# A hybrid encoder layer on one core: the input projection as seven half-size products, its operands made in the stage before

## What is computed

```python
h = rmsnorm(x, g_mix)                       # x: (2048, 1024)
proj = h @ w_in + b_in                      # w_in: (1024, 2304)
qa = rotary(proj[..., :s1].reshape(b, s, 8, 64), positions)
ka = rotary(proj[..., s1:s2].reshape(b, s, 2, 64), positions)
va, qb, kb, vb = ...                        # the other columns of proj: 128, 512, 512, 512
oa = window_sink_gqa(qa, ka, va, sinks)
ob = chunk_relbias_attention(qb, kb, vb, rel_bias)
mix = concat([rmsnorm(oa, g_grp_a), rmsnorm(ob, g_grp_b)])
x = x + mix @ w_out
x = x + memory_cross_attention(rmsnorm(x, g_cross), rmsnorm(mem, g_mem), w_cq, w_ckv, w_co)
h = rmsnorm(x, g_ffn)
x = x + (silu(h @ w_gate) * (h @ w_up)) @ w_down
out = rmsnorm(x, g_final)
```

## Time and profile before

| | |
|---|---|
| Median of 3 runs | 2958.81 us (2955.07 to 2966.77) |
| The profiled execution | 2957.17 us |
| Its span | 2955.4 us |
| TensorE matmuls, share of the span | 94% |
| `stage_products`, first to last matmul | 16.0 to 129.2 us |
| `stage_qkv`, first to last matmul | 133.7 to 575.2 us |
| Attention, first matmul | 595.4 us |

### The profile page before, as it was taken

The page is one execution under the profiler, slowest core; times in us unless marked ns, Lnnn a source line. Parts: engine busy times, 40 slices in busy tenths (PEclk is TensorE's granted clock), DMA queues, the critical chain, the costliest instruction groups (busy, mean ns, idle before and its releaser), DMA issues. The chain is left out here.

```text
span 2955.4 us, 39417 instructions
## 1 busy us (share of the span) xinstructions
PE 2789.1 (94%) x14112; PEld 2358.7 (80%) x14112; DVE 1601.4 (54%) x2913; ACT 1063.8 (36%) x2101; POOL 1052.2 (36%) x756
## 2 busy tenths in 40 slices
PE   7898999789999899799998799999999998999998
PEld 7787878689999788688887588888788887788876
DVE  3247447357779533233333566667766665655354
ACT  5433333256666322233332333334333332222242
POOL 6644444301000011312121555555555554453152
PEclk9999999989999899899999899999999999999999
DMA  7656666475665433212223433335433333744454
GB/s 237 224 185 216 220 233 220 137 181 138 161 161 122 156 133 135 111 61 75 86 75 120 158 107 99 98 100 177 137 107 107 95 105 120 268 147 140 146 172 129
DMA packets 244536, 428.48 MB, mean 145 GB/s; under 512 B 17792, under 2 KB 151424, under 8 KB 239104
## 3 DMA queue, kind: packets, MB, share of 16 engines
q1 hardware_dynamic: 211040, 364.72, 38.5%
q10 hardware_dynamic: 33312, 61.35, 7.0%
HBM read 285.50 MB, written 135.27 MB: 142 GB/s over the span
## 5 line engine op out<-in xcount | busy, mean ns | idle before, releaser
L50 PE MATMUL gu_acc<-gu_t,shared_m 128*128 128x512 f32 x880 | 344.2, 391 | 8.6 <-DVE gu_t L2348 5.1
L51 PE MATMUL gu_acc<-gu_t,shared_m 128*128 128x512 f32 x880 | 343.5, 390 | 0.0
L52 PE MATMUL gu_acc<-gu_t,shared_m 128*128 128x512 f32 x880 | 343.4, 390 | 0.0
L334 POOL TENSOR_TENSOR front_wq_lo<-front_wq_raw,front_wq_hi 128x1024 fp32r<-128x1024 f32 x72 | 177.8, 2471 | 215.2 <-ACT front_wq_hi L330 214.7
L1424 PE MATMUL att_sum_o<-att_v,att_turned_sb 128*128 128x64 f32 x1616 | 204.2, 271 | 0.0
L50 PEld LDWEIGHTS gu_acc<-gu_t,shared_m 128*128 128x128 f32 x880 | 165.8, 188 | 44.6 <-issue 5.5
L1424 PEld LDWEIGHTS att_sum_o<-att_v,att_turned_sb 128*128 128x128 f32 x1616 | 198.5, 194 | 0.2
L52 PEld LDWEIGHTS gu_acc<-gu_t,shared_m 128*128 128x128 f32 x880 | 165.9, 189 | 34.7
L51 PEld LDWEIGHTS gu_acc<-gu_t,shared_m 128*128 128x128 f32 x880 | 166.0, 189 | 34.3
L1394 PE MATMUL att_sum_s<-att_k,att_q 128*128 128x320 f32 (+3 forms) x704 | 146.7, 328 | 25.1 <-DMA att_k<-qk_d 24.1
L2296 ACT ACTIVATE shared_m<-gu_w_sum 128x512 fp32r<-128x512 f32 x132 | 83.3, 631 | 226.0 <-PE gu_acc L52 210.6
(11 more groups left out here) (310 smaller groups left out, 7335.5 us busy)
## 6 DMA issues: line engine op xcount, KB each, us to landing
front_wq_raw<-in_w_in ACTq DMA_DIRECT2D x69, 512.0 KB, 3.8
down_a<-a_d SPq DMA_DIRECT2D x37, 704.0 KB, 4.1
ahead_w_even<-in_w_gate SPq DMA_DIRECT2D x44, 512.0 KB, 4.4
more_w_odd<-in_w_up SPq DMA_DIRECT2D x44, 512.0 KB, 4.3
a_d<-gu_a_mix SPq DMA_DIRECT2D x88, 256.0 KB, 3.1
att_k<-qk_d SPq DMA_DIRECT2D x36, 512.0 KB, 13.1
a_d<-gu_a SPq DMA_DIRECT2D x66, 256.0 KB, 4.1
shared_m<-a_d SPq DMA_DIRECT2D x19, 704.0 KB, 4.3
```

What stands on the lines that cost most here:

```text
L50: pe.matmul(out, l_hi, r_hi, start=first, stop=False)
L51: pe.matmul(out, l_hi, r_lo, start=False, stop=False)
L52: return pe.matmul(out, l_lo, r_hi, start=False, stop=last)
L334: pool.tensor_tensor(self.lo[:, i % Q_SLOTS, :], self.raw[:, i % Q_SLOTS, :], raw(self.hi[:, i % Q_SLOTS, :]), ALU.subtract).then_inc(self ...
```

## The change

The projection is done by seven products of half depth for a pair of column tiles and half of the tokens (`N_PROD`, `PAIRS_IN`), 18 such pairs in all, 126 products of 12 matmuls. The columns of `w_in` are ordered anew outside of the kernel, so that a rotation pairs results of two tiles (head halves lie in different tiles): the four swap DMAs are gone, GpSimd makes the sine products (`sin_products`), VectorE the cosine products and the sums (`rotate`). GpSimd also makes the sums of weights (`sums`). A pair of weight tiles is loaded once per half of the tokens instead of once per block of 512. The stored q and k have 14 tiles of columns where there were 13.

All sixteen row tiles of x are now prepared in `stage_products`, as whole float32 tiles `prod_h` (no high and low there); VectorE forms four mixtures of each two (`mix_pair`), and the seven operands go to DRAM as `th_d` (56 stores of 256 KB, 24 from ScalarE and 32 from SyncE). They are loaded back in `stage_qkv`, as 14 operands of 1 MB, the first two ahead of its start (`FirstOperands`, which also serves the gate and up stage in place of `GateUpOperands`, with the same operations). The sine and cosine table is made once, in `stage_products`, and stored to `trig_d`. The rows of x have four buffers instead of two; ScalarE issues their loads and the stores of the unmixed operands. `m_d` is stored in rows of 4 KB and read back in four pieces.

```diff
     def load(self, sp, n, rows):
-        if n >= 2:
-            sp.wait_ge(self.s_xn, n - 1)
-        sp.dma_start(self.x[:, n % 2, :], rows).then_inc(self.s_x[n % 2], 16)
+        if n >= self.slots:
+            sp.wait_ge(self.s_xn, n - self.slots + 1)
+        sp.dma_start(self.x[:, n % self.slots, :], rows).then_inc(self.s_x[n % self.slots], 16)
...
-        SQUARE, SCALE, TURN = (2, 6, 24, 40), (3, 7, 28, 41), (5, 14, 34, 43)
-        RSQRT, LOAD = (6, 10, 15, 19), (5, 5, 11, 15)
...
+        def at_share(share):
+
+            whole = sum(cost(a) for a in range(TOTAL))
+            return min(a for a in range(TOTAL) if sum(cost(i) for i in range(a + 1)) >= min(share, 1) * whole)
...
+        def stage_at(j, steps):
+            return at_share((8 + 5.6 * j + steps) / 106)
+
+        TURN = [stage_at(j, 0) for j in range(NT)]
+        SCALE = [stage_at(j, -3) for j in range(NT)]
+        SQUARE = [stage_at(j, -7) for j in range(NT)]
+        WHOLE = [stage_at(j, 2) for j in range(NT)]
+        MIX = [stage_at(2 * i + 1, 5) for i in range(HT)]
+        PUT_MIX = [stage_at(2 * i + 1, 9) for i in range(HT)]
+        AT_ONCE = rows.slots - MT
+        TABLE = [at_share((20 + 4 * part) / 106) for part in range(6)]
+        AHEAD = at_share(0.75)
...
+                def put_mixed(i):
+                    sp.wait_ge(s_mixed, 4 * i + 4)
+                    put(sp, 5, i, h[:, (2 * i + 1) % 4, 0:KH, :], s_plain[i % 2])
+                    for m, q in enumerate((3, 2, 4)):
+                        put(sp, q, i, mixed[:, i % 2 * 3 + m, :, :], s_mst[i % 2])
...
+                    dve.tensor_tensor(t3, h22, h12, ALU.subtract).then_inc(s_mixed, 1)
+                    dve.wait_ge(s_mixed, 4 * i + 1)
+                    dve.tensor_tensor(h12, h12, h11, ALU.subtract).then_inc(s_mixed, 1)
+                    dve.wait_ge(s_mixed, 4 * i + 2)
+                    dve.tensor_tensor(t2, h22, h12, ALU.subtract).then_inc(s_mixed, 1)
+                    dve.wait_ge(s_mixed, 4 * i + 3)
+                    dve.tensor_tensor(t4, t2, h21, ALU.subtract).then_inc(s_mixed, 1)
...
+                def load_x(j):
+                    rows.load(act, MT + j, rows_of(x, tile_of(j)))
+
+                def put_plain(j):
+                    i, z = divmod(j, 2)
+                    act.wait_ge(rows.s_lo, 2 * MT + 2 * j + 2)
+                    if z == 0:
+                        put(act, 0, i, h[:, j % 4, 0:KH, :], s_plain[i % 2])
+                        put(act, 1, i, h[:, j % 4, KH:KT, :], s_plain[i % 2])
+                    else:
+                        put(act, 6, i, h[:, j % 4, KH:KT, :], s_plain[i % 2])
+
...
+                def sums(kp):
+
+                    w = w_raw[kp % 2]
+                    w11, w12, w21, w22 = w[:, 0, 0:H], w[:, 0, H:D], w[:, 1, 0:H], w[:, 1, H:D]
+                    pool.wait_ge(s_w[kp % 2], 32 * (kp // 2) + 32)
+                    if kp >= 1:
+                        pool.wait_ge(s_wlo_s, len(SUMS) * kp)
+                    pool.tensor_tensor(w_sum[:, 0, :], w21, w22, ALU.add).then_inc(s_ws, 1)
+                    pool.wait_ge(s_ws, 4 * kp + 1)
+                    pool.tensor_tensor(w21, w11, w21, ALU.subtract).then_inc(s_ws, 1)
+                    pool.tensor_tensor(w_sum[:, 1, :], w_sum[:, 0, :], w11, ALU.subtract).then_inc(s_ws, 1)
+                    pool.wait_ge(s_ws, 4 * kp + 3)
+                    pool.tensor_tensor(w_sum[:, 2, :], w12, w_sum[:, 1, :], ALU.subtract).then_inc(s_ws, 1)
...
+                    for i, g in enumerate(reversed(ROTATE[z])):
+                        pool.tensor_tensor(turned_part[:, i, :], y[:, g, :], trig[:, 1, z, :], ALU.mult
+                                           ).then_inc(s_part, 1)
...
+                    for g in (a, b):
+                        dve.tensor_tensor(y[:, g, :], y[:, g, :], trig[:, 0, z, :], ALU.mult).then_inc(s_cos, 1)
+                    dve.wait_ge(s_cos, 2 * r + 1)
+                    dve.tensor_tensor(y[:, a, :], y[:, a, :], turned_part[:, 0, :], ALU.subtract).then_inc(s_rot, 1)
+                    dve.wait_ge(s_cos, 2 * r + 2)
+                    dve.tensor_tensor(y[:, b, :], y[:, b, :], turned_part[:, 1, :], ALU.add).then_inc(s_rot, 1)
...
+                    if q == 0:
+                        return
+                    dve.wait_ge(s_prod, s + 1)
+                    if q == 1:
+                        dve.wait_ge(s_p1, kp + 1)
+                        result(0, bank, p1[:, :], ALU.add)
+                    if q == 2:
+                        dve.tensor_tensor(u2[:, :], bank, p1[:, :], ALU.add).then_inc(s_sum, 1)
+                    if q == 3:
+                        ready(2)
+                        dve.tensor_tensor(u3[:, :], bank, u2[:, :], ALU.add).then_inc(s_sum, 1)
+                    if q == 4:
+                        ready(3)
+                        result(1, u3[:, :], bank, ALU.subtract)
+                    if q == 5:
+                        result(2, bank, u3[:, :], ALU.add)
+                        dve.tensor_tensor(u2[:, :], bank, u2[:, :], ALU.add).then_inc(s_sum, 1)
+                    if q == 6:
+                        ready(6)
+                        result(3, bank, u2[:, :], ALU.add)
...
+                for s in range(TOTAL):
+                    kp, q = split_at(s)
+                    if s >= ACCS:
+                        consumed(pe, s - ACCS)
+                    if q in PLAIN:
+                        pe.wait_ge(s_wlo_a, lows(s, PLAIN))
...
+                        pe.wait_ge(s_wlo_s, lows(s, SUMS))
+                    if kp % PAIRS == 0:
+                        pe.wait_ge(s_tlo, 2 * (kp // PAIRS * N_PROD + q) + 2)
+                    hi, lo = (part[q].rearrange("p (u k c) -> p k u c", k=KH, c=P) for part in (t_hi, t_lo))
+                    for k in range(KH):
                         wk = slice(k * P, (k + 1) * P)
+                        last = split3(pe, acc[s % ACCS][:, :].rearrange("p (u c) -> p u c", c=P), w_hi[s % RS][:, wk],
+                                      w_lo[s % RS][:, wk], hi[:, k], lo[:, k], k == 0, k == KH - 1)
+                    last.then_inc(s_prod, 1)
+                    for v in values_due(s):
+                        turn(v)
```

1083 lines of the change are left out of this document (601 added, 482 removed).

## The result

| | before | after |
|---|---|---|
| Median | 2958.8 us (11 runs, 2955.06 to 2966.77) | 2970.13 us (11 runs, 2964.03 to 2974.46) |
| Ratio | | 1.0035 (95% interval 1.0025 to 1.0045) |
| The profiled execution, its span | 2957.17, 2955.4 us | 2972.94, 2971.2 us |

The account below looks back on a forecast made before the run. TensorE's matmuls, over 94% of the span, were taken as the bound. Projection -69.3, rotated pairs +4, behind the projection -5 and first stage +38 make -32 against 2957.2: 2925, as a median 2927 us, range 2895 to 2975.

Parts of the forecast that it names:

- projection, 376.2 us: Projection: 372.2 us against 441.5, a gain of 69.3, with 4 us charged for six rotated pairs.
- behind the projection: Between projection and attention: the last pair is unrotated and takes 2.9 us instead of 8.1, priced at -5.
- first stage and barrier: First stage: 160 us for its bytes plus 11 us, so +38; bounds +10.4 and +115.
- later stages: Stages from attention on: same durations; a change by over 5 us would make the prediction wrong.
- lockstep: First stage: 11 us because engines in lockstep never keep DMA full, with first loads, last stores and barrier.
- the fourth: First stage stretches: in-order queues keep DMA at 235 GB/s, 78 us more, 3005 us; chance 0.16.
- cases 1 and 3: The terms as summed, chance 0.57; or rotated pairs hold up TensorE in the projection, 2960 us, chance 0.13.
- case 1: Whole kernel as summed, 2905 to 2950 us for first-stage rates of 385 to 315 GB/s; chance 0.57.
- The sum of 131 us for the port: First stage: the port pair shared by VectorE and GpSimd held 131 us, less than the sum by bytes.
- The matmuls' count and pace: Projection: 1512 matmuls instead of 1728, at 0.2267 us each, 342.8 us.
- One start and one change of halves: Projection: 18.4 us for start, change of halves and clock, taken whole from the gate and up stage.
- the case that priced them at 37: Projection: rotated pairs hold up TensorE for 37 us instead of 4, giving 2960 us; chance 0.13.

Follow-up runs that it names:

- e1: Changed kernel without the 24 stores of the mixtures for products 2, 3 and 4, which read product 5's operand instead; one execution, 2959.36 us.
- e9: e6 without the 24 stores of the mixtures for products 2, 3 and 4; one execution, 2951.17 us.
- e3: Changed kernel with the conversions of the projection's first operands made seven or eight accumulators later in the first stage; 2956.68 us, ratio to before 0.9992.
- e6: e3 with each row tile's square and scaling three steps earlier in the first stage; 2951.96 us, ratio to before 0.9974.
- e12: e3 with the projection's second half using the first half's operands, its 14 loads and their conversions left out; one execution, 2942.66 us.
- e7: e3 with the rotation computing one column of 512, instructions and waits kept; one execution, 2947.62 us, projection 384.8 us instead of 394.9.
- e11: Changed kernel with two buffers for rows in place of four; 2988.92 us, ratio to before 1.0091.
- e5: Changed kernel with the loads of x and the plain stores issued from SyncE, four buffers kept; 2964.14 us, ratio to before 1.0023.
- e10: e6 with the angle table's 17 VectorE instructions 16 of 106 steps earlier in the first stage; 2950.84 us, ratio to before 0.9968.

## Why the prediction was wrong

In the forecast's own terms, for the profiled executions:

| term | forecast | measured |
|---|---|---|
| projection, 376.2 us | -65.3 | -44.1 |
| behind the projection | -5 | -5.4 |
| first stage and barrier | +38 | +59.7 |
| later stages | 0 | +5.6, within the scatter |
| sum | -32 | +15.8 (medians +11.3) |

**The first stage** is 21.7 us longer than forecast. The step that failed is the one that priced it by bytes (55.9 MB at 350 GB/s). The bytes were right, 55.99 MB; the model was not. Leaving 6.3 MB out brought 8.8 us in e1 and 1.1 in e9, while moving instructions in the queues, with all bytes kept, brought 10.6 (e3) and 5.5 more (e6). These two make 16.1 of the 21.7 us. What stretches the stage are late hand-offs: a scaled row behind a burst of VectorE's other work, and ScalarE before operands that have not landed. I had added 11 us for "lockstep" beside the bytes, where it is the main term. With both moved (e6), 5.6 us over the forecast are left, and they lie in the end: 10.7 us from the last product to the projection, where I took 4.5 from before, because the last evictions stand behind VectorE's low parts.

Of the cases the fourth comes nearest: in-order queues keep the rate down, deciding under 291 GB/s, and the stage runs at 290. But its body, 3005 us and a start at 210 or later, did not come, only the part that falls short, to which the forecast gave 0.04, and its place is wrong. It named SyncE's loads behind waits for mixtures, which are 6.0 us in all. The waits are VectorE's and ScalarE's. That 2970 lies within the range is luck: the range was made for cases 1 and 3, and neither came. The 2905 to 2950 of case 1 do not follow from its rates either: 55.9 MB at 385 and 315 GB/s are 145 and 177 us, so 2912 to 2945.

That VectorE and GpSimd disturb each other, cited as a rule of the Trainium skill (SBUF — State Buffer, section "SBUF: two separate sides"), is seen in the trace: two-input operations of 0.69 us take up to 2.8 while GpSimd subtracts. The sum of 131 us for the port was rightly not the largest term, as the stage takes 172. But the disturbance has a part in the hand-offs that came late: the 32 mixtures take 36.9 us where 32 x 0.69 = 22.1, and 11.1 of the 32.8 us of the burst above are due to such long operations. How much of TensorE's waiting would go with it is open.

**The projection** gains 21.2 us less. The matmuls' count and pace were right. Some 2 of the 21.2 us are the scatter of this one execution. Two sizes were off. "One start and one change of halves", 18.4 us from the gate and up stage, was too small: the change of halves alone is 14.7 (e12), and the start has 10.0 us of waits besides (2.4 and 7.7), as five of the first seven operands are loaded only after the barrier. The rotated pairs cost 10.1 us and not 4 (e7); the case that priced them at 37 was the right mechanism, at a quarter of its size. Together: 342.8 + 11.0 + 14.7 + 10.1 = 378.6; the 18.8 that are left to 397.4 are a remainder, with the start, its clock and the scatter in it. That the two effects, each measured on e3, add up was not measured.

**Behind the projection** -5.4 for -5: right, by its own steps. The last store is issued at 593.6, 2.8 us after the last product, for 2.9 forecast and 8.1 before.

The forecast of no change in later stages holds; the 4.9 us before the gate and up stage exceed neither its bound of 5 nor the scatter.

**Two parts of the change** by themselves: four buffers are worth 24 us of the first stage and 19 us of the median (e11); issuing from ScalarE is worth nothing (e5). With the conversions and scalings moved (e6), and the table too (e10), the change does gain, 0.3% over before, some 8 to 10 us where 32 were forecast.

## What to carry to other kernels

When work is moved into a stage whose engines hand each row on several times (square, factor, scaling, transposes, copy, mixture, store), the sum by bytes or by busy time is a floor and not the price: look at where in each in-order queue the new instruction stands, and what bursts stand ahead of it. A conversion of operands "ahead" belongs where its load has surely landed; put earlier, it blocks the engine for the stage that is still running (10.6 us here). A single-buffered set of operands, loaded again at half time, is a second start, and it is priced from its own bytes.

## What the hardware showed unexpectedly

- The DMA queues keep 393 to 429 GB/s for some 19 us (e6, 153 to 172 us), more than the 386 that I had for the best rate.
- TensorE's waits come with a lower granted clock for the matmuls around them. In the first stage of the changed kernel TensorE's matmuls are busy for 124.9 us; in e6, with 14 us less standing still, the same matmuls are busy for 117.3, at a granted clock of 0.89 for 0.86. In the window of 40 us around the change of halves TensorE's clock was 0.87 with the waits and 1.00 without them.
- A stretch of the same code, between attention's first matmul and the gate and up stage's, differs by up to 7.3 us between executions of kernels that do not touch it.
